# Attention probabilities scaled before their transposes, with the second values moved behind the next scores

## The reference

```python
def sink_probs(scores, mask, sinks):
    sc = jnp.where(mask, scores, NEG_INF)
    sink = sinks.astype(jnp.float32).reshape(N_KV_HEADS, Q_GROUP, 1, 1)
    m = jnp.maximum(jnp.max(sc, axis=-1, keepdims=True), sink)
    p = jnp.exp(sc - m)
    denom = jnp.sum(p, axis=-1, keepdims=True) + jnp.exp(sink - m)
    return p / denom
...
    p = sink_probs(scores, mask, sinks).astype(vv.dtype)
    o = jnp.einsum("bnkgqs,bnskd->bnqkgd", p, vv).reshape(b, s, ATTN_WIDTH)
```

## Time and profile before

| what | value |
|---|---|
| median of 3 runs | 905.67 us (905.65 to 905.95) |
| the profiled execution | 904.12 us, its span 902.1 us |
| TensorE busy | 875.0 us, 97% of the span |
| VectorE, ScalarE, GpSimd busy | 559.2, 400.9, 252.1 us |
| granted clock of TensorE, mean | 0.993 |
| one turn of the attention loop | 16.5 us |

### The profile page before, as it was taken

The page is one execution under the profiler, slowest core; times in us unless marked ns, Lnnn a source line. Parts: engine busy times, 40 slices in busy tenths (PEclk is TensorE's granted clock), DMA queues, the critical chain, the costliest instruction groups (busy, mean ns, idle before and its releaser), DMA issues. The chain is left out here.

```text
span 902.1 us, 16890 instructions
## 1 busy us (share of the span) xinstructions
PE 875.0 (97%) x5635; PEld 782.7 (87%) x5636; DVE 559.2 (62%) x1025; ACT 400.9 (44%) x732; POOL 252.1 (28%) x250
## 2 busy tenths in 40 slices
PE   7999999999999999999999999999899999999995
PEld 7777776888999999999999999999778888888884
DVE  5687775543489655565434955445887758577561
ACT  5667665310254443333211222213527657577461
POOL 2434332344230000000002530000153456454562
PEclk9999999999999999999999999999899999999998
DMA  8433431350532322223973138863458988989833
GB/s 282 141 95 117 128 77 36 98 216 2 211 102 71 142 96 96 96 96 128 345 265 96 50 118 282 307 213 92 155 163 305 339 266 301 332 235 324 288 46 58
DMA packets 79553, 153.55 MB, mean 170 GB/s; under 512 B 10702, under 2 KB 44174, under 8 KB 78961
## 3 DMA queue, kind: packets, MB, share of 16 engines
q1 hardware_dynamic: 72000, 134.84, 43.2%
q0 software_dynamic: 7488, 17.85, 8.7%
HBM read 122.80 MB, written 40.30 MB: 181 GB/s over the span
## 5 line engine op out<-in xcount | busy, mean ns | idle before, releaser
L1493 POOL TENSOR_TENSOR hT_lo_raw<-hT_lo_raw,arena 128x1056 f32<-128x1056 f32 x7 | 23.3, 3328 | 226.7 <-DVE arena L1739 226.7
L2489 DVE TENSOR_TENSOR hT_lo<-room,hT_hi (+1 forms) x32 | 72.2, 2293 | 17.1 <-ACT hT_hi L2178 17.1
L79 PE MATMUL psum<-w_hi,hT_hi 128*128 128x512 f32 (+3 forms) x216 | 79.1, 366 | 1.7 <-DVE hT_lo L1112 1.0
L79 PE MATMUL psum<-hT_hi,x_xT_hi 128*128 (+1 forms) x192 | 77.9, 406 | 1.5 <-DVE x_xT_lo L2641 0.7
L80 PE MATMUL psum<-hT_lo,x_xT_hi 128*128 (+1 forms) x192 | 75.8, 395 | 0.0
L81 PE MATMUL psum<-hT_hi,x_xT_lo 128*128 (+1 forms) x192 | 75.8, 395 | 0.0
L81 PE MATMUL psum<-w_hi,hT_lo 128*128 128x512 f32 (+3 forms) x216 | 75.2, 348 | 0.0
L80 PE MATMUL psum<-w_lo,hT_hi 128*128 128x512 f32 (+3 forms) x216 | 75.2, 348 | 0.0
L2118 POOL DMA_INDIRECT out_y<-y,put_at x23 | 47.0, 2043 | 92.2 <-DMA out_y<-y,put_at 78.2
L2178 ACT ACTIVATE hT_hi<-room (+1 forms) x32 | 59.9, 1924 | 11.5 <-PE psum L81 10.1
L1533 ACT ACTIVATE arena<-arena 128x264 f32<-128x264 f32 x64 | 26.9, 426 | 75.7 <-DVE arena L1728 75.1
(11 more groups left out here) (414 smaller groups left out, 2631.9 us busy)
## 6 DMA issues: line engine op xcount, KB each, us to landing
room<-in_w_gu SPq DMA_DIRECT2D x16, 2048.0 KB, 11.4
dn_raw<-in_w_dn SPq DMA_DIRECT2D x16, 1024.0 KB, 7.0
arena<-in_w_ab SPq DMA_DIRECT2D x24, 512.0 KB, 4.5
gate_rows<-arena SPq DMA_DIRECT2D x32, 264.0 KB, 2.4
arena<-gate_rows SPq DMA_DIRECT2D x16, 528.0 KB, 3.8
xT_chunk<-in_xT SPq DMA_DIRECT2D x8, 528.0 KB, 4.1
x_in<-in_x SPq DMA_DIRECT2D x8, 512.0 KB, 5.4
h_rows<-h_raw SPq DMA_DIRECT2D x8, 512.0 KB, 4.0
```

The lines of the kernel that those rows point to most:

```text
L79: eng.matmul(out, lh, rh, start=first and k == 0, stop=False)
L1493: pool.tensor_tensor(here, here, part[v % 2], ALU.add).then_inc(h2_summed, 1)
L2489: dve.tensor_tensor(gu_lo[:, buf, ks], gu_raw[:, buf, ks], gu_hi[:, buf, ks].bitcast(F32), ALU.subtract).then_inc(gu_lo_made.sem, 1)
```

## The change

Each group's probabilities are multiplied by 1/(den + sink_e) before they are transposed. ScalarE does this in place with a copy that has a scale per row (scale_probs, four instructions a group), after VectorE has made the four reciprocals of the group (invert_dens, now per group and without the widening). What values puts into bank 5 is then normalised, so that dens_turn, copy_rT and o_scale are gone, and oa_high and oa_low read bank 5 itself. values(t, 0) therefore waits for oa_low of the tile before it. The copy of the second pT moves from ScalarE to VectorE.

The order of each turn changes as well. On TensorE the second probs_turn moves behind the last piece of project_q, and scores(s, 0) and spread_rstd(s + 2) come ahead of values(s - 1, 1). On ScalarE the first exponentials come ahead of copy_kv, each group's scalings follow its exponentials (copy_kv between them for the first group), and both stand ahead of h_high. On VectorE invert_dens(0) stands ahead of the second masking, oa_low behind it, and the second copy of pT between k_scale and the sum of the queries' squares.

```diff
@@ probs, ScalarE
                 if t >= 1:
-                    act.wait_ge(rd_made, t)
+                    act.wait_ge(rd_made, u - 1)
...
-            def copy_second_pT(t):
...
-            def copy_rT(t):
...
+            def scale_probs(t, gp):
+                k0 = block_keys(t)
+                act.wait_ge(rd_made, 2 * t + gp + 1)
+                for kv, i, j, g in heads_of(gp):
+                    ins = act.activation(p_sb[:, gp, j, k0:], p_sb[:, gp, j, k0:], ACT.Copy, scale=rden[:, gp, j:j + 1])
+                ins.then_inc(p_scaled, 1)
 
             def oa_high(t):
                 if t < PT:
-                    act.wait_ge(o_scaled, t + 1)
-                    src = o_n
+                    act.wait_ge(o_made, 2 * t + 2)
+                    src = bank(psum, 5)
...
                 if s == PT:
                     probs(done, 0)
+                    scale_probs(done, 0)
+                    probs(done, 1)
                     copy_q(s)
-                    probs(done, 1)
+                    scale_probs(done, 1)
                     copy_kv(s)
-                    copy_second_pT(done)
                     vs_high(0)
-                    copy_rT(done)
...
                 else:
                     if s > 0:
+                        probs(done, 0)
                         copy_kv(s)
-                        probs(done, 0)
+                        scale_probs(done, 0)
                         probs(done, 1)
+                        scale_probs(done, 1)
                     h_high(s + 1)
-                    if s > 0:
-                        copy_second_pT(done)
...
-                    if s > 0:
-                        copy_rT(done)
@@ probs_turn and values, TensorE
-                pe.wait_ge(p_made, u + 1)
+                pe.wait_ge(p_scaled, u + 1)
...
                 if t >= 1:
-                    pe.wait_ge(o_scaled, t)
+                    pe.wait_ge(oa_lo_made, t)
@@ the loop, TensorE
                 probs_turn(s - 1, 0)
                 project_q(s, 4, 6)
                 values(s - 1, 0)
+                project_q(s, 6, KD)
                 probs_turn(s - 1, 1)
-                project_q(s, 6, KD)
-                values(s - 1, 1)
                 qk_turn(s)
-                dens_turn(s - 1)
+                scores(s, 0)
                 if s + 2 < NT:
                     spread_rstd(s + 2)
-                scores(s, 0)
+                values(s - 1, 1)
@@ VectorE
-            def invert_dens(t):
-                dve.wait_ge(p_made, 2 * t + 2)
...
-            def o_scale(t):
...
+            def invert_dens(t, gp):
+                dve.wait_ge(p_made, 2 * t + gp + 1)
+                step.did(dve.tensor_tensor(rden[:, gp, :], den[:, gp, :], sink_e[:, gp, :], ALU.add))
+                dve.reciprocal(rden[:, gp, :], rden[:, gp, :]).then_inc(rd_made, 1)
...
                 mask_scores(done, 0)
                 if s + 1 < NT:
                     h_scale(s + 1)
+                invert_dens(done, 0)
                 mask_scores(done, 1)
+                if done >= 1:
+                    oa_low(done - 1)
...
                 copy_pT(done, 0)
+                invert_dens(done, 1)
                 if s == PT:
                     q_squares(s)
                     k_squares(s)
                 else:
                     k_scale(s)
-                if done >= 1:
-                    oa_low(done - 1)
-                invert_dens(done)
+                copy_pT(done, 1)
...
-                o_scale(done)
```

More of the change, by code:

```diff
@@ L165, in attention_phase @@
         s_sb, p_sb = sp_sb[:, 0], sp_sb[:, 1:]
-        rT, o_n = (sp_sb[:, 0, 2 * n:2 * n + 2, :].rearrange("p g c -> p (g c)") for n in range(2))
         z, _ = brief((("z_qkv", [P, AW + KVW]), ("behind_z", [P, G * KV * HD])))
@@ L804, in values @@
                 mm.then_inc(o_made, 1)
-            def dens_turn(t):
-                pe.wait_ge(rd_made, t + 1)
-                pe.wait_ge(z_copied, q_count(t + 1))
-                for gp in range(2):
-                    for i in range(2):
-                        g = 2 * gp + i
-                        mm = pe.transpose(bank(psum, 0)[:, g * P:(g + 1) * P], o_sb[:, g, :, :].rearrange("p k d -> p (k d)"),
-                                          ident[:, :])
-                mm.then_inc(rT_made, 1)
             def sample_scores():
@@ L943, in _ @@
             values(PT - 1, 1)
-            dens_turn(PT - 1)
             qk_turn(PT)
@@ L1077, in copy_pT @@
                                 psum[:, 6 + first:8, :].rearrange("p a c -> p (a c)")).then_inc(pT_copied, 1)
-            def invert_dens(t):
-                dve.wait_ge(p_made, 2 * t + 2)
-                if t >= 1:
-                    dve.wait_ge(rT_made, t)
-                a, b = (x[:, :, :].rearrange("p a (k i) -> p a k i", i=2) for x in (den, sink_e))
-                step.did(dve.tensor_tensor(rden[:, :, :].rearrange("p a (i k) -> p a k i", k=KV), a, b, ALU.add))
-                step.did(dve.reciprocal(rden[:, :, :], rden[:, :, :]))
-                dve.tensor_copy(o_sb[:, :, :, :].rearrange("p g k d -> p (g k) d"),
-                                rden[:, :, :].rearrange("p a n -> p (a n)").unsqueeze(2).broadcast_to([P, HEADS, HD])).then_inc(rd_made, 1)
-            def o_scale(t):
-                dve.wait_ge(o_made, 2 * t + 2)
-                dve.wait_ge(rT_copied, t + 1)
-                dve.tensor_tensor(o_n, bank(psum, 5), rT, ALU.mult).then_inc(o_scaled, 1)
+            def invert_dens(t, gp):
+                dve.wait_ge(p_made, 2 * t + gp + 1)
+                step.did(dve.tensor_tensor(rden[:, gp, :], den[:, gp, :], sink_e[:, gp, :], ALU.add))
+                dve.reciprocal(rden[:, gp, :], rden[:, gp, :]).then_inc(rd_made, 1)
             def oa_low(t):
                 dve.wait_ge(oa_hi_made, t + 1)
-                src = o_n if t < PT else bank(psum, 4)
+                src = bank(psum, 5 if t < PT else 4)
                 dve.tensor_tensor(oaT[1][:, :, toks(t)],
```

17 lines of the change are left out of this document (2 added, 15 removed).

## The result

| | before | after |
|---|---|---|
| median of the runs, us | 905.66 (904.57 to 905.95) | 921.75 (919.22 to 922.47) |
| profiled execution, us | 904.12 | 921.77 |
| its span, us | 902.1 | 919.8 |

The changed kernel takes 1.0175 of the time before, 95% interval 1.0154 to 1.0196: 16.1 us more by the medians, where 9.8 was forecast. 921.75 lies in the range given (910 to 926), but above the forecast's own range (912 to 920.5).

The account below looks back on a forecast made before the run. TensorE, busy 875.0 of 902.1 us, was taken as the bound. First turn +2.9, five full turns +6.2, seventh +1.0 and last -0.3 gave +9.8 us, so 915.5 us from the 905.67 median; range 910 to 926.

Parts of the forecast that it names:

- the range given: Whole kernel: 910 to 926 us, holding the forecast and one to three clock falls, 0.8 together.
- the forecast's own range: Whole kernel without clock falls: 912 to 920.5 us around 915.5, chance 0.74.
- What bounds, and where the change is decided: Attention loop: TensorE sets the time, helpers have 4 to 5 us slack a turn; TensorE's waits for helpers decide.
- The hole: Ahead of scores(s, 0): TensorE idle 2.07 us a turn, awaiting VectorE's copy, squares, kT copy; net +1.24 a turn.
- The spread: Spreading matmul behind the scores on TensorE: between 0.2 and 0.39 us, taken as 0.2.
- The scalings: ScalarE's eight a turn, 0.37 to 0.51 us each: just hidden; at 0.51 showing up to 0.5 a turn.
- The first turn: Loop's first turn: transposes stall 1.3 us for scalings, later work delayed again; +2.9, between +1.5 and +3.5.
- The seventh and the last turn: Loop's end: seventh, without a spreading matmul, +1.0 us; last -0.3, bounds -1.0 to +1.5, its 1.11 wait remaining similar.
- The sum: Attention loop: first turn +2.9, five full turns +6.2, seventh +1.0, last -0.3, in all +9.8 us.
- one to three falls: Rival, chance 0.07: TensorE's clock falls to 0.50 around the idle time, 3.4 us each, giving 919 to 926 us.
- The rule on transposes: Second transposes to scores: transposes not counting as busy, 3.5 us looks idle, a fall every turn; 939 us, chance 0.04.
- What follows the loop is TensorE's own work with little waiting: Stages behind the attention loop: the loop's delay, +9.8 us, reaches the kernel's end.

Follow-up runs that it names:

- the kernel with 12 transposes: Changed kernel plus 12 identity transposes into bank 0 between qk_turn and scores(s, 0) each turn; 918.44 us (1.0164), profiled execution 915.03.
- without the scalings: Changed kernel with ScalarE's eight scalings a turn left out, reciprocals and waits kept; 911.40 us (1.0081), whole time not comparable since routing differs; turns 17.83.
- kernels with the keys first: Changed kernel with qk_turn ahead of second transposes, keys' copy ahead of second pT copy; second kernel also has that copy on ScalarE; 910.81 and 909.63 us.
- GpSimd early: Changed kernel with keys first and second pT copy on ScalarE, plus GpSimd's h subtractions ahead of its roots; 909.18 us (1.0044).
- the old order: Changed kernel with TensorE's order of the kernel before, keeping the scalings and VectorE's changed order; 921.96 us (1.0182), turns 18.27.
- the values first: Changed kernel with values(s - 1, 1) moved behind qk_turn(s), ahead of the spread and scores(s, 0); 911.25 us (1.0066), turns of 17.0.
- the copy on ScalarE: Changed kernel in the keys-first order, with the second pT copy also back on ScalarE behind the copies of q; 909.63 us (1.0048).
- the 6 matmuls: Changed kernel plus 6 fp32 identity matmuls into bank 0 between qk_turn and scores(s, 0) each turn; 916.02 us (1.0133), turns 17.83.
- its reordered version: Kernel before, normalisation behind the values and no scalings, in the keys-first order with second pT copy on ScalarE behind q's copies; 901.93 us (0.9968).
- the one with 12 matmuls: Changed kernel plus 12 fp32 identity matmuls into bank 0 between qk_turn and scores(s, 0) each turn; 923.48 us (1.0199), turns 19.08.

## Why the prediction was right, and where it was wrong

**What bounds, and where the change is decided.** Right: TensorE at 97% before, helpers with slack, and the cost in TensorE's idle time at one place.

**The hole.** Right in its chain, 3.44 us for 3.52, and in the turn, 17.83 for 17.8. The spread was put at 0.2 and holds TensorE for 0.41. The view's idle time ahead of the scores, 1.37 us, is under the 1.7 to 2.1 named as a sign, by the other way of counting. The size is shown by filling it (17.83 stays 17.83) and by the two orders that move work into it (17.02, 16.24).

**The scalings.** Right: hidden in full turns (17.83 without them). The sum took them at 0.37 each, with 0.51 as the other end. Four lasted 1.71 together, spaced about 0.4, near the low end.

**The first turn.** Forecast +2.9. The transposes came at 35.51 after 1.28 of waiting for the scalings (forecast 35.6 and 1.3), and the next turn's projection started 2.9 late (45.47 for 42.6). Right.

**The seventh and the last turn.** The seventh was put at +1.0; undisturbed, in the kernel with 12 transposes, it took 17.74 against 16.52, +1.2. For the last the forecast was -0.3. From scores(7, 0) to sample_v_parts that kernel takes 17.63 us, the kernel before 16.83, and 1.02 of second values has moved into the stretch: -0.2. The wait ahead of the last second values stays, as forecast, with 1.32 for the 1.11 of the earlier trace rows:

```profile
172.04 1.08 PE L788 MATMUL psum<-pT,v_ring 128*64 128x256 f32 x8 [1.32 <-DVE pT L1050]
```

**The sum.** +9.8 forecast for the loop, +9.96 and +10.1 measured where the clock stayed up. The step that failed is another one.

**The step that failed: the clock.** The prediction put one to three falls at 0.07, as a rival that excludes the forecast, and named a full clock as a sign of being right. Three falls occurred in the profiled execution, and they cost 6.0 us of its 17.7. That 921.75 lies within 910 to 926 is luck on this side: the range was drawn wide enough for a rival that was hardly believed. The argument against it was that a wait of 1.11 behind transposes had left the clock alone in the earlier trace rows, and that the fall before had a longer stretch. The forecast's own hole was 2.07, as long as the 1.99 that preceded that fall, and there was one in each of seven turns. A forecast that creates such waits has to carry the falls in its sum. It would have had to say 915.5 plus one to three falls.

The price was mis-sized too: 1.57, 3.06 and 1.35 us for the three, not 3.4 each. The fall that it was read from cost nothing. The changed kernel has the same wait of 1.99 at the same place, and there the clock stayed up:

```profile
654.80 3.84 PE L2371 MATMUL psum<-ident 128*128 128x128 f32 x32 [1.99 <-POOL yT L2067]
661.76 0.54 PE L2383 MATMUL psum<-c_marks,c_lower 128*128 128x160 f32 x2 [3.13 <-DVE yT L2552]
```

The 32 products took 3.84 us instead of the 6.66 of the earlier trace rows, and the next work of the stage came 6.96 us after their start; before, with the fall, it was 6.98, because TensorE waits there for VectorE. All thirteen traces have this wait, and twelve of them a fall behind it. Why the changed kernel's trace is the one without is open; one execution doesn't tie it to the kernel.

Over the attention loops of all thirteen traces TensorE waited 40 times for 1.05 to 1.32 us in one piece, and no fall followed. Of 18 waits between 1.36 and 2.38 us, 8 were followed by one: three of six in the changed kernel, two of six without the scalings, and of the six others the 1.93 of both kernels with the keys first and the 2.18 with GpSimd early, but not the 2.24 and 2.38 in the first turns of the two, nor a 1.55 in the old order. So inside the loop only the longer waits were followed by a fall, and not each of them; which one is, is open.

An idle TensorE isn't the only thing that a fall can follow. Between 185 and 199 us, behind the loop, four traces have one more, with TensorE busy all the time: those of the values first, of TensorE's old order, of the copy on ScalarE and of the 6 matmuls. In the first of them (two rows of TensorE, then the stretches):

```profile
184.37 1.07 PE L880 MATMUL psum<-lg,vs 32*128 32x32 f32 x8
185.38 2.00 PE L823 MATMUL psum<-h_raw,pT_spread 128*128 128x64 f32 x16
```

```profile
186.00:187.00 1.00, 1.00 (x12) 1.00 (x11) 0.71 (x3) 0.00 (x0) 0.14 (x1) 1.00 0.00 0
188.00:189.00 1.00, 1.00 (x3) 0.82 (x3) 0.00 (x0) 0.00 (x0) 0.92 (x1) 0.50 0.00 0
```

In all four the same three us of narrow products (32x32, 128x64) stand ahead of it. The changed kernel and the one before have this work too, and no fall there.

**The rule on transposes.** The Trainium skill, TensorE: Matmul & The Clock Gate, Part 4 (PE-mode transpose), was cited for the view that transposes don't count as busy, by which every turn would have fallen. The trace speaks against it: with the hole filled by 12 more transposes TensorE has 3.4 us of transposes only, some 0.3 of waiting among them, in each of seven turns, and the clock stayed at 1.00 in all of them in the profiled execution, just as with matmuls. In the changed kernel three of seven such places had a fall. This is one trace against one; the mean granted clocks given with the fillings point the same way.

**"What follows the loop is TensorE's own work with little waiting."** Nearly: 1.8 us more came there, 1.5 of them at the start of the dense stage. Four loads are issued together there, at 231 us before and at 247 after. The rows show ScalarE's rounding of the last load in the kernel before, then the same in the changed kernel, with a wait of TensorE that follows from it:

```profile
243.03 1.06 ACT L1501 ACTIVATE first_u_hi<-first_u_raw 128x1024 fp32r<-128x1024 f32 x1 [4.88 <-DMA first_u_raw<-in_w_tiles]
```

```profile
260.40 1.06 ACT L1466 ACTIVATE first_u_hi<-first_u_raw 128x1024 fp32r<-128x1024 f32 x1 [6.43 <-DMA first_u_raw<-in_w_tiles]
275.65 0.36 PE L79 MATMUL psum<-hT_hi,w_hi 128*128 128x264 f32 x1 [1.13 <-DVE w_lo L1615]
```

This load took 12.1 us from issue to landing, 10.5 before, and two of the other three were late by as much (9.1 for 7.6, 11.4 for 9.8). All that ScalarE and VectorE did behind them came 1.5 us later in the stage, and TensorE lost that in two pieces, at 262.83 and at 275.65. The wait at 275.65 stands in the changed kernel and in nine of its ten variants, and neither in the kernel before nor in its reordered version; the exception is the one with 12 matmuls. The load goes with it: from the first issue to ScalarE's start it is 12.0 to 12.1 us in the three traces without the wait, and 13.2 to 13.6 in the ten with it. So the late loads make the wait; why they are late was not tried and is open, as is the remaining 0.3.

**My own forecasts for the runs.** The turns of six orders were foretold to within 0.15 us (17.02, 17.66, 18.27, 16.24, 16.04 and 16.08), but the times of the two kernels with the keys first by 7 us too low, since their first turns (16.7 and 16.6 us against 14.83), the block between VectorE and GpSimd, the fall behind it and the late loads had no place in the sum. The old order on TensorE came out 3 us over its 918.8, the 12 matmuls 7 over the 916.5 given, as they outlast the hole, the 12 transposes 2 over it, and GpSimd early 1 over its range.

## What to carry to other kernels

- When a change drops work from the bound engine, look first at what filled that engine while its helpers finished. Here 0.44 us of transposes a turn went, and 1.65 us of standing still came, because the work behind the helpers' chain was put behind the operation that waits for it. An order that gives TensorE other work while the helpers' chain runs was worth 1.6 us a turn with the scalings (17.83 to 16.24) and 0.44 without (16.52 to 16.08), as much as the removed work or more.
- A forecast that makes TensorE wait in one piece for as long as places where the clock fell must carry the clock in its own sum: here 8 of 18 waits of 1.36 to 2.38 us were followed by a fall. And read what a fall cost at the place where you take its price from: the one before cost nothing.
- Price the moved step in the first and the last turn by themselves. Steady turns hid the scalings entirely; the first turn paid 1 us and more for them.

## What the runs showed of the hardware

**GpSimd holds VectorE up.** VectorE's 128x4 addition lasted 2.56 us, and its 128x4 negation 1.12, beside GpSimd's SBUF to SBUF subtractions, each to within 0.03 us of their end; 0.16 and 0.17 without. With the subtractions moved away, the addition was short in every turn. Masks that read PSUM kept their 0.54 beside the same subtractions. The Trainium skill, SBUF — State Buffer, "SBUF: two separate sides", says that the two share a port pair under an exclusive lock for an instruction's whole length, also against VectorE operations with two SBUF inputs. The traces agree for the addition, which has two. The negation has one, and was held all the same; and the addition was held over two subtractions, not one. Within one program a shift of less than 0.1 us decided: started 0.1 ahead of the subtractions the addition was short, started 0.03 ahead it was held.

**The price of a fall.** From 1.00 to 0.50 for 3.4 us, 1.35 and 1.57 us lost; once for 6.8 us, 3.06 lost. Nothing was lost where TensorE had to wait for VectorE anyway (6.98 us with the fall, 6.96 without).

**Fp32 identity products.** 12 matmuls of 128x128 are 24 instructions and 2.84 us, 12 transposes of the same data 1.47 us.
